# Turning and scaling the hidden rows tile by tile between two layers, and part of them earlier at the start

## The reference

```python
shift1, scale1, gate1, shift2, scale2, gate2 = jnp.split(mod, 6, axis=-1)
h = rmsnorm(x, norm1_g) * (1 + scale1) + shift1
aq, ak, av, bq, bff, bfb, bv, bg, cq, ck, cv, du = jnp.split(h @ w_in, offsets, axis=-1)
...
h2 = rmsnorm(x, norm2_g) * (1 + scale2) + shift2
x = x + gate2 * moe(h2.reshape(bsz * l, -1), ...)
```

## Time and profile before

| | us |
|---|---|
| median of 3 runs (1279.88 to 1282.71) | 1281.07 |
| the profiled execution | 1280.95 |
| its span, first to last instruction | 1279.1 |
| TensorE busy | 1187.2 (93%) |
| VectorE busy | 522.3 (41%) |
| ScalarE busy | 429.5 (34%) |
| GpSimd busy | 229.7 (18%) |

### The profile page before, as it was taken

One profiled execution on the slowest core, in us unless ns is written; L12 is line 12 of the kernel. 1 busy time (PEld: TensorE's weight loads), 2 busy tenths in 40 slices (PEclk: granted clock), 3 DMA queues, 4 the chain that ended last, 5 costly groups with the idle time before them and its releaser, 6 DMA issues.

```text
span 1279.1 us, 19883 instructions
## 1 busy us (share of the span) xinstructions
PE 1187.2 (93%) x7830; PEld 542.6 (42%) x7830; DVE 522.3 (41%) x1267; ACT 429.5 (34%) x740; POOL 229.7 (18%) x339
## 2 busy tenths in 40 slices
PE   4999899899899999999989989988998999999994
PEld 1555555454433333333354655555444333333331
DVE  1384667733522122111365747575244122122217
ACT  2223444431332333333421434352222432333333
POOL 1230274210011110010200325441200011110000
PEclk9999889889899999999999998997998999999997
DMA  9839531565799999999740312055715999999971
GB/s 364 298 145 167 108 99 66 214 230 226 299 345 407 386 388 386 395 388 381 285 177 1 140 66 92 8 215 217 304 56 207 361 397 385 399 393 388 393 299 80
DMA packets 52242, 324.79 MB, mean 254 GB/s; under 512 B 7825, under 2 KB 8241, under 8 KB 33600
## 3 DMA queue, kind: packets, MB, share of 16 engines
q1 hardware_dynamic: 39296, 293.16, 59.2%
q0 software_dynamic: 11584, 25.79, 8.1%
q10 hardware_dynamic: 1280, 4.72, 0.9%
HBM read 318.50 MB, written 24.09 MB: 268 GB/s over the span
## 4 chain that ended last, share of the span: by engine, by line
PE 71%; DVE 14%; DMA 10%; issue 2%; ACT 1%; SPq 0%; DVEq 0%; ACTq 0%; POOLq 0%
PE ps L1944 33%; PE ps L1577 12%; DMA ring<-moe_w_up 7%; PE ps L1633 7%; PE ps L1834 7%; PE ps L1593 3%; DVE attT L1174 3%; PE ps L1933 3%; PE ps L1616 2%; DMA ring<-ada_w 2%; DVE dbuf L1151 2%; PE ps L1728 1%; DVE small L1279 1%; PE ps L1757 1%; DVE dbuf L1146 1%
## 5 line engine op out<-in xcount | busy, mean ns | idle before, releaser
L1944 PE MATMUL ps<-ring,dbuf 128*32 128x512 f32 x3072 | 426.0, 593 | 4.2 <-DMA ring<-moe_w_up 1.9
L1944 PE MATMUL ps<-extra,dbuf 128*32 128x512 f32 x1536 | 206.6, 592 | 1.9 <-DMA ring<-moe_w_up 1.9
L1944 PEld LDWEIGHTS ps<-ring,dbuf 128*32 128x32 f32 x3072 | 118.4, 110 | 199.9 <-issue 194.2
L1577 PE MATMUL ps<-ring,extra 128*128 128x512 f32 (+1 forms) x384 | 149.0, 548 | 0.0
L1944 PEld LDWEIGHTS ps<-extra,dbuf 128*32 128x32 f32 x1536 | 60.2, 110 | 131.8 <-issue 131.6
L1000 ACT ACTIVATE big<-ps 96x512 f32<-96x512 f32 x32 | 34.5, 1077 | 224.1 <-issue 167.5
L1633 PE MATMUL ps<-extra,ring 128*128 128x384 f32 x320 | 108.9, 499 | 0.0
L759 POOL DMA_INDIRECT expert_rows<-big,lst x28 | 26.3, 941 | 427.2 <-DVE big L1457 411.8
L1577 PEld LDWEIGHTS ps<-ring,extra 128*128 128x128 f32 x384 | 73.7, 193 | 69.3 <-issue 65.8
L1435 DVE COPY dbuf<-ps 128x384 f32<-128x384 f32 x32 | 17.8, 558 | 200.2 <-PE ps L1933 200.2
L1834 PE MATMUL ps<-ring,extra 128*128 128x512 f32 x192 | 84.3, 594 | 3.0 <-DVE extra L1344 1.8
(11 more groups left out here) (280 smaller groups left out, 1460.6 us busy)
## 6 DMA issues: line engine op xcount, KB each, us to landing
ring<-moe_w_up SPq DMA_DIRECT2D x30, 2048.0 KB
ring<-ada_w SPq DMA_DIRECT2D x24, 2048.0 KB
ring<-moe_w_down SPq DMA_DIRECT2D x18, 2048.0 KB
ring<-moe_w_gate SPq DMA_DIRECT2D x16, 2048.0 KB
extra<-moe_w_gate SPq DMA_DIRECT2D x16, 2048.0 KB
extra<-moe_w_down SPq DMA_DIRECT2D x14, 2048.0 KB, 18.0
ring<-w_in SPq DMA_DIRECT2D x12, 2048.0 KB
ring<-w_out SPq DMA_DIRECT2D x4, 2048.0 KB
```

The source lines that it names most:

```text
L1577: ins = pe.matmul(out, a, b, start=(n == 0), stop=(n == len(pairs) - 1))
L1944: return pe.matmul(p[QT * g:QT * (g + 1), :], a, w, start=start, stop=stop, tile_position=(0, QT * g))
```

## The change

- At the end of layer 0, `returned` goes tile by tile: both late experts for tile 0, then tile 1, then tile 2. The wait for the last expert's rows moves up behind `returned(0, 0)`.
- Between the layers a tile is turned as its norm is done (`turned_tile`): two banks of four chunks, for one tile. Three useless products stand ahead of tile 0 and four ahead of tile 1 (nine in one go before). A half of four chunks is scaled by `modulate_half` with four instructions of 128x128: ACT takes both halves of tile 0 ahead of tile 2's sum of squares, and then the second halves of tiles 1 and 2; DVE takes the first halves of tiles 1 and 2 behind the last `normalize`. `z` waits at its first matmul for the first half of all three tiles, at its fifth for the second halves.
- `scales` for layer 1 moves to where the modulation is ready, ahead of layer 0's experts.
- In layer 0 the first six chunks are turned behind the second modulation block, in place of one useless product; one useless product fewer follows the third block. `z`'s first product starts ahead of chunks 6 and 7, which are turned between its sixth and seventh matmul.
- Banks are dealt out anew for these jobs.

```diff
+EARLY_CHUNKS = 6
+TILE_BANKS, AFTER_TILES = [5, 0, 1, 3, 6, 2], 4
 def layer_jobs(l):
-    jobs = [("mod", 0)] if l == 0 else []
-    jobs += [("hT", 2 * l, k) for k in range(KC)]
+    if l == 0:
+        chunks = [("hT", 0, k) for k in range(KC)]
+        jobs = chunks[0:EARLY_CHUNKS] + [("mod", 0), z[0]] + chunks[EARLY_CHUNKS:] + z[1:]
+    else:
+        jobs = z
...
+            def modulate_half(l, t, b):
+                act.wait_ge(s_mod, 2 * l + 1)
+                job, s = ("hT", 2 * l, t, b), min(t, 1)
+                p = ready(act, job)
+                for n in range(4):
+                    k = 4 * b + n
+                    ins = act.activation(hT[:, k, t * P:(t + 1) * P], p[:, n * P:(n + 1) * P], ACT.Identity, ...)
+                    if n < 3:
+                        step(ins)
+                release(act, ins, job)
...
-                sum_squares(2 * l)
                 if l == 0:
+                    sum_squares(0)
                     rows_out(0)
-                modulate(l)
+                    modulate(0)
+                else:
+                    squares_of(2 * l, 0)
+                    squares_of(2 * l, 1)
+                    modulate_half(l, 0, 0)
+                    modulate_half(l, 0, 1)
+                    squares_of(2 * l, 2)
+                    modulate_half(l, 1, 1)
+                    modulate_half(l, 2, 1)
...
-                scales(l, 0)
-                modulate(l)
+                    scales(0, 0)
+                    modulate(0)
+                else:
+                    modulate_half(l, 1, 0)
+                    modulate_half(l, 2, 0)
...
                     modulation(group(*AHEAD[l][-1]))
+                    scales(l + 1, 0)
...
+            def turned_tile(l, t):
+                pe.wait_ge(s_xn, NT * 2 * l + t + 1)
+                for b in range(2):
+                    transposes(("hT", 2 * l, t, b), [xn[:, t, k * P:(k + 1) * P] for k in range(4 * b, 4 * b + 4)])
...
-                    if job[0] == "z":
-                        moved(pe, ("hT", 2 * l, k))
+                    if job == ("z", 0, 0, 0):
+                        if k == EARLY_CHUNKS:
+                            hidden(range(EARLY_CHUNKS, KC))
+                        moved(pe, ("hT", 0, k))
+                    if job == ("z", 1, 0, 0) and k % 4 == 0:
+                        for t in range(NT):
+                            moved(pe, ("hT", 2, t, k // 4))
...
-                    for j, n in zip(ADA_FIRST, (3, 1, 2, 0)):
+                    for j, n in zip(ADA_FIRST, (3, 0, 1, 0)):
                         mod_rows(0, j)
+                        if j == 1:
+                            hidden(range(EARLY_CHUNKS))
                         keep_running(n, MOD_BANK - 1)
                     mod_turn(0)
-                hidden(2 * l)
...
-                for t in range(2):
+                for t in range(NT):
                     for b in range(2):
                         begin(pe, ("cm", l, t, b))
                     returned(t, 0)
-                for kind in ("dn0", "dn1"):
-                    moved(pe, (kind, l), NE - 1)
-                returned(0, 1)
-                returned(1, 1)
-                for b in range(2):
-                    begin(pe, ("cm", l, 2, b))
-                returned(2, 0)
-                returned(2, 1)
+                    if t == 0:
+                        for kind in ("dn0", "dn1"):
+                            moved(pe, (kind, l), NE - 1)
+                    returned(t, 1)
                 if l < L - 1:
-                    keep_running(9)
+                    keep_running(3)
+                    turned_tile(l + 1, 0)
+                    keep_running(4)
+                    turned_tile(l + 1, 1)
+                    turned_tile(l + 1, 2)
```

More of the change, by code:

```diff
@@ L139, in layer_jobs @@
 def layer_jobs(l):
-    jobs = [("mod", 0)] if l == 0 else []
-    jobs += [("hT", 2 * l, k) for k in range(KC)]
-    jobs += [("z", l, d, hp) for d in range(2) for hp in range(HP)] + [("aqk", l, t) for t in range(NT)]
+    z = [("z", l, d, hp) for d in range(2) for hp in range(HP)]
+    if l == 0:
[3 more added lines that the diff above has]
+        jobs = z
+    jobs += [("aqk", l, t) for t in range(NT)]
     jobs += [("bq", l, 0), ("bq", l, 1)] + [("av", l, t) for t in range(NT)] + [("bvg", l, t) for t in range(NT)]
@@ L168, in place_jobs @@
     for l in range(L):
+        if l:
+            for i, b in enumerate(TILE_BANKS):
+                uses[b] += 1
+                place[("hT", 2 * l, i // 2, i % 2)] = (b, uses[b])
+            n = AFTER_TILES
         for job in layer_jobs(l):
@@ L805, in rows_out @@
                 act.activation(rows, ps[:, MOD_BANK, :], ACT.Copy).then_inc(free[MOD_BANK], 1)
+            def modulate_half(l, t, b):
[4 more added lines that the diff above has]
+                    k = 4 * b + n
+                    ins = act.activation(hT[:, k, t * P:(t + 1) * P], p[:, n * P:(n + 1) * P], ACT.Identity, scale=A1[:, 0, k, s:s + 1],
+                                         bias=modv[:, l, k, s:s + 1])
+                    if n < 3:
+                        step(ins)
+                release(act, ins, job)
             def modulate(l):
@@ L1103, in scales, with modulate_half @@
                 dve.wait_ge(s_mod, 2 * l + which + 1)
+            def modulate_half(l, t, b):
+                job, s = ("hT", 2 * l, t, b), min(t, 1)
+                p = ready(dve, job)
+                for n in range(4):
+                    k = 4 * b + n
+                    ins = dve.tensor_scalar(hT[:, k, t * P:(t + 1) * P], p[:, n * P:(n + 1) * P], A1[:, 0, k, s:s + 1],
+                                            modv[:, l, k, s:s + 1], ALU.mult, ALU.add)
+                    if n < 3:
+                        step(ins)
+                release(dve, ins, job)
             def modulate(l):
@@ L1617, in transposes, with hidden @@
                 fill(ins, job)
[L1619 to L1622, removed]
+            def hidden(chunks):
+                pe.wait_ge(s_xn, NT)
+                for k in chunks:
+                    transposes(("hT", 0, k), [xn[:, t, k * P:(k + 1) * P] for t in range(NT)])
+            def turned_tile(l, t):
+                pe.wait_ge(s_xn, NT * 2 * l + t + 1)
+                for b in range(2):
+                    transposes(("hT", 2 * l, t, b), [xn[:, t, k * P:(k + 1) * P] for k in range(4 * b, 4 * b + 4)])
             def by_token(l, w, job, t, c0, c1):
```

## The result

The changed kernel takes 1286.12 us (median; five of its six executions lie between 1285.19 and 1286.89) against 1281.38 for the kernel before: ratio 1.0036, 95% interval 1.0022 to 1.0049. The sixth execution, a slow one, took 5802.22 us and has no part in the ratio. The change is slower by some 4.7 us, above the range of the prediction (1284.9) and beyond the 2.6 us that the prediction took for the least that can be told from no change.

What follows compares the result with a forecast made beforehand. The prediction took TensorE's chain to bound the kernel nearly throughout. Start +2.9, passage between the layers -0.2 and end -1.7 summed to +1.0, a median of 1282.0 us, range 1278.6 to 1284.9 for 8 in 10.

Steps and rivals of the forecast that it cites:

- the start: Start of layer 0, early chunks and `z`: +2.9 us, bounds +0.9 and +4.5.
- the passage: Between the layers, from returned products to layer 1's `z`: -0.2 us, bounds -1.9 and +1.1.
- Part 1: Returned products tile by tile: DVE's first add 1.76 us sooner, the end -1.7; the wait for rows holds by 0.2.
- Part 3, step 4: Start of layer 0: TensorE idles before `z`, its clock falls and `z` runs at half speed: +1.5 us.
- the case of two prices: Rival: clock falls twice at the start, the second on block four or `mod_turn`; start +4.5, total 1284.5; chance 0.20.
- Part 3, step 3: Inside layer 0's `z`: six transposes, 0.67, and 0.9 waiting for DVE at chunk 6; first product ends +1.4 us.
- Step 2: Start of layer 0: `z` begins at 40.4 when its weights land, 0.2 us sooner, bounds 0 and 0.7.
- Part 2, step 5: Between the layers: clock falls before layer 1's `z`, at like price on both sides; -0.2 us, bounds -1.9 and +1.1.
- steps 1 to 4: Between the layers: two scalings in series eat the 1.7 us gained; `z` starts 0.2 sooner at like clock.
- no new clock cost arises: Rival: the clock costs nothing new at the start or between the layers; total -0.5, 1280.5 us; chance 0.15.
- the clock stays up into `z` of layer 1: Rival: useless products keep the clock between the layers, -1.9 there; total -2.1 to -2.7, about 1278.6 us; chance 0.10.
- the start's delay is absorbed by the waits for weights: Rival: layer 0's expert weights come at their old time, ending the start's delay; total -1.9, 1279.1 us; chance 0.10.

Runs made afterwards that it cites:

- e12: The changed kernel run once more, unaltered: 1285.22 us, ratio 1.0022 to the kernel before.
- e6: Changed kernel with the old start and five more useless products around the turned tiles between the layers: 1279.26 us, ratio 0.9972.
- e4: Changed kernel with five more useless products at the start, ahead of block four and behind `mod_turn`: 1282.37 us, ratio 1.0001.
- e1: Kernel before with only the start's part of the change: 1286.50 us, ratio 1.0031.
- e8: Changed kernel with chunks 6 and 7 turned ahead of layer 0's `z`, and more useless products behind block three and `mod_turn`: 1280.11 us, ratio 0.9992.
- e9: Kernel before with thirteen useless products in place of nine between the layers: 1279.67 us, ratio 0.9982.
- e10: e6 with tile 2's squares ahead of ACT's second half of tile 0: 1277.39 us, ratio 0.9963.
- e11: Changed kernel with the start of e8 and the useless products of e6 between the layers: 1279.09 us, ratio 0.9978.
- e2: Changed kernel with the old start, keeping the new products' order and passage between the layers: 1281.71 us, ratio 0.9994.
- e7: e3 with eleven useless products in place of nine between the layers: 1276.01 us, ratio 0.9946 to the kernel before.
- e5: Changed kernel with two more useless products behind the third modulation block only: 1285.63 us, ratio 1.0025.
- e3: Kernel before with only the new order of the returned products: 1277.78 us, ratio 0.9969.

## Why the prediction was wrong

The forecast was +1.0, with the start at +2.9, the passage at -0.2 and the end at -1.7. The profiled execution gave +4.45, +0.32 and -1.72, and +1.1 in the stretches that the change leaves alone. Of the 3.16 that its span lies above the forecast, 1.55 is the start, 0.52 the passage, and 1.11 is in C and F, where its cause stays open. In e12 the span grew by 2.7: the start is 0.65 over, the passage 1.26, and C and F are 0.18 shorter. Its +2.8 by the median would lie within the forecast's range (-2.5 to +3.8 about 1281.07), the +4.7 of the first comparison lies above it.

**Part 1 held.** DVE's first add comes 1.71 us sooner behind the returned products, its idle 1.76 is gone, and the end is 1.7 shorter in every trace with the new order (G, 24.58 to 24.60, against 26.30 to 26.32). The wait for the last expert's rows didn't bite here; its margin of 0.2 was thin, and in e6, one of eleven traces with the new order, it cost 0.4 between the layers.

**Part 3, step 4, the price of the low clock at the start, is the step that failed.** I took one price, 1.5, and gave the case of two prices 0.20. The profiled execution shows that rival's cost, +4.45 for its +4.5, though in one low stretch from 34.90 to 45.00 and not in two falls. A is 0.79 later through block four (+0.99) and `mod_turn` (+0.82), and A to B takes 8.50 where e4 takes 6.69, so 1.81 more inside `z`: 2.60 in all where I had 1.5. I had named its condition, the idle stretch ahead of block four that one useless product fewer leaves. The 18 early transposes, which the prediction counts in favour of a kept clock, don't cover that stretch: they end at 28.1 (25.94 + 2.19 in that timeline), and from 31.0 to 34.0 TensorE has 1.03 us of work. But e1 and e12 have the like idle stretch (2.01 and 1.70) without a fall there, so the condition alone doesn't decide it. Where the fall comes only in `z` (e1, e12), it costs 1.52 and 1.70; the 1.5 was right for that case, and the start is then +3.32 and +3.55, still above +2.9, chiefly by step 3.

**Part 3, step 3 was under-sized.** Six transposes and the wait for chunk 6 were put at 0.67 + 0.9 = 1.57, and the sum took +1.4 because `z` was to start 0.2 sooner. e4 and e8 show up to 1.85, and `z` starts at 40.54 and 40.59 in e1 and e12, no sooner than before. Step 2's 40.4 for the landing of the weights lies within what the traces show, but `z`'s start moves with the transfers: in nine traces (e1 to e6, e9, e10, e12) it comes 6.46 to 6.51 behind the first product of block four, and A lies between 39.82 and 40.59.

**Part 2, step 5 failed as well; steps 1 to 4 held to within 0.4.** ACT's squares behind eight scalings, and DVE's scalings in series behind the last norm, eat what the products gain: with the clock kept on both sides E is 29.54 and 29.91 (e11, e6) against 29.50 (e9), 0.0 to +0.4 where I had -0.2. But the fall isn't of like price on both sides. In the six traces of the new passage with its clock falling, E lies between 31.23 and 32.61, and the fall costs `z` 1.70 to 3.07; in the old passage it cost the transposes 1.56. (The prediction's 1.73 for these sets the whole group of layer 1, 4.40, against the 2.67 that the chain shows of layer 0's; in the timeline that group runs from 37.93 for 2.82, which leaves 1.58.) The upper bound of +1.1 allowed for one price more, but e2 has +1.55.

**The other rivals.** That no new clock cost arises (-0.5) is what e4 comes near, +0.23 by its median, and there it took five more useless products. That the clock stays up into `z` of layer 1 was priced at -1.9 for the passage; e6 and e11, where it does, show -1.15 and -1.52. That the start's delay is absorbed by the waits for weights falls with e1: C is 589.90 there and 590.23 before, but F is 2.06 longer, within what F scatters, and the median has all of the delay.

The Trainium skill ("TensorE: Matmul & The Clock Gate", Part 1) holds that the ramp isn't worth fitting at under 1% of a kernel. In share of time the traces agree: one fall is 1.5 to 3 us of 1280, 0.1 to 0.2%. For this change they speak against leaving the falls out, since with them it is slower (e12), without the one at the start it can't be told from the kernel before (e4), and without both, and without the wait inside `z`, it is faster (e11).

**What stays open.** The +1.28 in C of the profiled execution isn't there in e12 (590.52), so I don't put it down to the change; what makes C and F scatter wasn't tried, and neither was why the first comparison has 4.7 and the second 2.8 (their intervals overlap). Nor do the traces settle why the clock of the same kernel fell in block four in one profiled execution and only in `z` in the other.

## What to carry to other kernels

When transposes are moved out of a wait, ask what kept TensorE's clock up in that wait: work that is free can still be what the next product's speed rests on, and useless products in its place cost little here. A fall is priced by what runs in the low stretch, so ask it of every idle stretch that comes before long products. And work put inside a chain of products, however short, brings its partner's latency with it: six transposes of 0.82 us cost up to 1.85. Turning and scaling tile by tile cost 1.77 against scaling chunk by chunk beside the transposes (e11, e7), 0.70 of it by the order of ACT's queue alone (e10). The gain was in the simplest parts: the order of the products and two useless products more (e7).

## What the runs showed of the hardware

- One profiled execution of the changed kernel stood at a granted 0.50 from 34.90 to 45.00, and the other fell only in `z` (1.00 from 37 to 40, 0.67 from 40.4 to 43); the fourth block's products took 2.89 us in the one and ran at full clock in the other, with TensorE's work the same.
- Two useless products more ahead of block four didn't keep the clock up in `z` (e5, 6.53 us for twelve records, against 5.66 in e1 without them); with useless products behind `mod_turn` too it stayed at 1.00 (e4, 4.14 for the same records).
- Between the layers the low clock cost nothing while TensorE turned single tiles (D 24.62 or 24.63 with and without it) and 1.70 to 3.07 in the product behind them.
- Four useless products more between the layers of the kernel before took 1.56 us from the passage and 2.7 from the median (e9, ratio 0.9982, 0.9967 to 0.9997).
- The same code took between 589.46 and 592.76 us in four profiled executions (C in before, e3, e7, e9), a spread as large as the effects that were looked for.
